# Attention scores in two passes over stacked rounded parts, part stores one chunk later in the queue, first head fetched a stage early, latent keys in two column tiles

## The chip, the cores and the metric

The kernel runs on one NeuronCore of a Trainium2 chip. The metric is the device time of one execution in microseconds (us), the median of the runs. TensorE multiplies matrices and writes to PSUM; VectorE, ScalarE and GpSimd work elementwise; SP's queue issues nearly all transfers. All data are 32-bit floats. A float32 product of TensorE is exact to float32 and leaves two records in the trace; a product on the rounded type float32r leaves one, and the kernel gets its precision back by cutting an operand into a rounded high part and the rounded rest (low part) and adding products of parts.

## The reference

Two transformer blocks run one after the other on x of 1024 tokens by 1024 channels. The first has differential and latent attention, a memory attention and a mixture of experts. What the change touches there is the up-projection of latent keys, `(_rms_norm(c_kv) @ w_mla_ukv)`, 8 heads of 64 key rows. The second block projects its normalised input with `w_in` into rows for four mixers and gates:

```python
fq, fk = rms_norm(fq, fox_q_gain), rms_norm(fk, fox_k_gain)         # 4 heads of 64
c = cumsum(log_sigmoid(f_logit))                                    # per head, over tokens
s = q @ k.T * d**-0.5 + (c[i] - c[j]); causal; softmax; @ v         # fox_attention
mlstm: (q @ k.T) * exp(decay), causal, 4 heads; sum over keys; rms_norm; * sigmoid(mo)
sq, sk = rms_norm(...)                                              # 8 query heads, 2 key heads
s = q @ k.T * d**-0.5 + bias, keys of the last 128 tokens; softmax with sink; @ v   # swa_attention
y_conv = short_conv_mixer(cu, cb, cc, conv_w)
g = sigmoid(gates); merged = sum over 4 branches of g * (y @ w_branch); x = x + merged @ w_merge
```

A SwiGLU feed-forward network ends the block.

## The kernel before, in words

P = 128, S = 1024, HD = 64, HALF = 512, ST = 8 token blocks of 128. Stages follow one another with a barrier between them. Three matter here.

`first_rows` (L1097) makes the rows of the first mixer. TensorE multiplies one chunk of 128 output rows after the other, each as 48 products of parts, and puts the work of one latent head into the middle of a chunk (`head`): four float32 products of 512 columns for the queries, into `q_ps` (L1250), two for the keys, into partitions 0 to 63 of `k_ps` (L1253). ScalarE copies both out (`leave_head`, L1317 and L1318).

`mixer_rows` (L2963) projects 22 chunks of 128 rows for the second block: chunk 0 the gate logits, 1 to 4 fox queries and keys, 5 to 9 window queries and keys (1 to 9 are normalised), 10 to 19 plain, 20 and 21 output gates. For chunk j ScalarE rounds the weights (`high_part`, L3168), VectorE makes the low part (`low_part`, L3227), TensorE runs 48 products into `acc[j % 2]` (L235 to L237). A normalised chunk is squared by ScalarE (L3179), TensorE sums the squares per head (L3111, in the middle of the next chunk), VectorE scales the mean (L3232), ScalarE takes logarithm and exponential (L3189, L3191), VectorE writes the chunk to `stage[j % 2]` (`normalise`, L3239), and TensorE waits for that before chunk j + 2. ScalarE's program for chunk j is: leave(j), rounding of the weights of j + 2, roots of j. VectorE's is: low part of the weights of j + 2, mean, normalise, then parts of the gate rows (`gate_step`, behind chunks 0, 5, 9 and 10) and sums of token blocks (`block_sum`, L3305). SP's program is the loop

```python
for j in range(2, N):
    load(j)              # waits for low part j - 2, then 512 KB of weights
    if j >= 3:
        store(j - 2)     # waits until chunk j - 2 is in its stage
```

with the stores of gate rows, window rows and token blocks between. GpSimd is idle in this stage after some fills.

`gated_attention` (L3654) runs 128 steps of one block of 128 queries: steps 0 to 31 fox heads, 32 to 63 recurrent (mLSTM) heads, 64 to 127 window heads, head g = step // 8. In one step TensorE makes the score of the block (`score`, L4000), transposes the exponentials of the step before, runs its share of the gate projection (`gates`, L235 to L237, some ten products of 512 columns) and multiplies with the values (L4020) or, for recurrent heads, adds up (L4031). A fox or recurrent score of block t is 128 by (t + 1) x 128 or S - t x 128 keys, a window score 128 by 256 (128 in block 0). It is float32, 64 channels and two more rows deep; for fox heads the two rows carry the running sum c of the query and of the key and ones, for others zeros, written once by GpSimd (L3970). The operands lie in `k.X` (`q_of`, `k_of`), in two sets by turns; `load_head(g)` (L3841) fills them through SP's queue, four transfers for fox heads and two for others, at step 8 (g - 1), after the scores of head g - 2. Head 0 and 1 and the gate memory `ml_y` are loaded at the start of the stage. VectorE shifts or weighs the scores (L4232, L4251), ScalarE exponentiates. SP also carries gate weights (L3861), gate stores and partial sums (L3883, L3891), convolution rows (L3919), token blocks (L3906) and the first two branch weights into `vm` (L3846, step 70).

`merge_branches` (L4360) follows and begins with the branch weights in `vm` and `fox_y`.

Of the kernel before, what the change touches and what calls it, by code (L numbers as in the profile page):

```python
# [22 lines left out]
F32 = mybir.dt.float32  # L23
# [96 lines left out]
class Core:  # L120


    def __init__(self, nc, ctx, dram, out, scratch):
# [29 lines left out]
        self.first_gate_in = ctx.enter_context(nc.semaphore("first_gate_in"))  # L153
        self.block_sums = ctx.enter_context(nc.semaphore("token_block_sums"))
# [13 lines left out]
        with ExitStack() as overlaid:  # L168
            self.sb("x_first_half", [P, ST // 2, D], ctx=overlaid)
            self.down_parts = pair(self, "moe_down_ws", [P, 2 * D], overlaid)  # L170
        self.X = sb("X", [P, ST, D])
# [925 lines left out]
def first_rows(k, H, vm, heads):  # L1097
# [4 lines left out]
    with k.phase() as ctx:  # L1102
# [119 lines left out]
        def _(pe):  # L1222
# [17 lines left out]
            def head(h):  # L1240
# [47 lines left out]
        def _(act):  # L1288
# [21 lines left out]
            def leave_head(h):  # L1310
# [6 lines left out]
                nc.scalar.activation(ks[b], k_ps[0:NOPE, :], ACT.Copy).then_inc(nopes, 1)  # L1317
# [1645 lines left out]
def mixer_rows(k, HT, vm, biases, sinks, spare, raw):  # L2963
# [11 lines left out]
    N_NORMED = 9  # L2975
    with k.phase() as ctx:
        weights = [pair(k, f"pr_ws{b}", [P, KD, P], ctx) for b in range(2)]
        stage = [k.sb(f"pr_stage{b}", [P, S], ctx=ctx) for b in range(2)]
# [10 lines left out]
        raws, logs, ones, a, top, floor, neg = ([k.X[0:H, c, :] for c in range(3)], [k.X[0:H, c, :] for c in (3, 4)],  # L2989
                                                k.X[0:H, 5, :], k.X[0:H, 6, :], k.X[0:H, 7, :],  # L2990
                                                spare[1][0:H, 0, :], spare[1][0:H, 1, :])
        totals = [spare[2][0:H, 0, :], spare[2][0:H, 1, :]]
        acc = [k.ps(f"pr_acc{b}", [P, S], ctx) for b in range(2)]
# [5 lines left out]
         wb_stored, wb_loaded, wb_turns, upright) = k.sems(  # L2999
            "pr", "cleared highs lows products left_normed left_plain stored0 stored1 squared summed meaned rooted bias_in "  # L3000
            "copied absed logged rows_made turned row_stored rel_in bucketed wb_made hot_made wb_product wb_rows "
            "wb_stored wb_loaded wb_turns upright")
# [22 lines left out]
        def _(sp):  # L3025
# [5 lines left out]
            def store(j):  # L3031
                sp.wait_ge(*left(j))
                sp.dma_start(chunks[j][2], stage[j % 2][:]).then_inc(stored[j % 2], 16)

            def store_rows():
                fox_q = k.scratch["fox_q"].rearrange("(h n) s -> h n s", n=2)
                fox_k = k.scratch["fox_k"].rearrange("(h n) s -> h n s", n=2)
                sp.wait_ge(cleared, 2)
                sp.dma_start(fox_q[:, 0, :], ones).then_inc(row_stored, 16)
                sp.dma_start(fox_k[:, 1, :], ones).then_inc(row_stored, 16)  # L3040
                sp.wait_ge(rows_made, 4)
# [2266 lines left out]
```

## Time and profile before

| what | value |
|---|---|
| median of 3 runs | 3204.66 us (3198.21 to 3834.82) |
| the profiled execution | 3198.8 us, span 3197.0 us |
| TensorE busy | 3001.7 us, 94% of the span |
| VectorE, ScalarE, GpSimd busy | 1985.1, 1567.1, 488.2 us |
| `mixer_rows` | about 1466 to 1752 us of the span |
| `gated_attention` | about 1752 to 2325 us of the span |

Busy time is the time in which an engine has an instruction under way; matmuls are pipelined, so the start-to-start distance of two tells what one costs, and its duration holds the way through the array too. PE is TensorE, PEld its weight loads, DVE is VectorE, ACT ScalarE, POOL GpSimd, SPq the queue of SP. "[9.85 <-PE x]" behind a row is idle time before it and what ended it.

### The profile page before, as it was taken

How to read it: one execution, taken by the hardware profiler on the slowest of the kernel's cores; microseconds unless marked ns; L12 is line 12 of the kernel's file. 1: busy time of each engine (PE TensorE's matmuls, PEld its weight loads, DVE VectorE, ACT ScalarE, POOL GpSimd, SP SyncE). 2: the span in 40 equal slices, each digit the busy share in tenths (PEclk: the TensorE clock that was granted, in tenths of full speed). 3: DMA queues.
4: the chain of work that ended last, by engine and by line, in shares of the span. 5: the costliest groups of instructions: out<-in, count | busy, mean ns of one | idle time of the engine just before them, and what ended most of it. 6: DMA issues, size and time to landing. Idle time of an engine off the chain costs nothing. (4 is left out here: it accounts for less than half of the span.)

```text
span 3197.0 us, 40651 instructions
## 1 busy us (share of the span) xinstructions
PE 3001.7 (94%) x14913; PEld 2468.0 (77%) x14913; DVE 1985.1 (62%) x2873; ACT 1567.1 (49%) x2494; POOL 488.2 (15%) x429
## 2 busy tenths in 40 slices
PE   7998999898969999969999999989999899999999
PEld 6766999686858878868777787778877778888887
DVE  4336888523678888873432434566576576666685
ACT  5225778533558888853521443344453432322443
POOL 0001210000133333220000110113300032222000
PEclk9999999899979999989999999999999999999999
DMA  3334221302168888772243433377664223333653
GB/s 113 85 122 125 60 60 31 112 20 102 66 248 294 298 287 299 248 236 66 79 133 98 114 99 109 106 233 219 193 240 151 79 80 103 111 113 116 230 159 112
DMA packets 299781, 459.71 MB, mean 144 GB/s; under 512 B 47799, under 2 KB 195326, under 8 KB 287042
## 3 DMA queue, kind: packets, MB, share of 16 engines
q1 hardware_dynamic: 274946, 411.72, 40.4%
q10 hardware_dynamic: 9088, 28.58, 2.3%
q0 software_dynamic: 15552, 16.82, 1.8%
q8 instruction: 121, 1.98, 0.3%
q14 instruction: 74, 0.61, 0.1%
HBM read 401.47 MB, written 118.98 MB: 163 GB/s over the span
## 5 line engine op out<-in xcount | busy, mean ns | idle before, releaser
L2850 DVE TENSOR_TENSOR moe_wgu_low<-moe_raw,moe_wgu_high 128x2048 fp32r<-128x2048 f32 x94 | 211.2, 2288 | 47.4 <-ACT moe_wgu_high L2787 45.3
L235 PE MATMUL ga_gate<-second_h_high,ga_ws_high 128*128 128x512 f32 x448 | 198.0, 442 | 12.6 <-DVE ga_ws_low L4189 10.4
L2787 ACT ACTIVATE moe_wgu_high<-moe_raw 128x2048 fp32r<-128x2048 f32 x92 | 171.2, 1909 | 20.2 <-ACT moe_y L2796 20.2
L237 PE MATMUL ga_gate<-second_h_high,ga_ws_low 128*128 128x512 f32 x448 | 180.7, 403 | 0.0
L236 PE MATMUL ga_gate<-second_h_low,ga_ws_high 128*128 128x512 f32 x448 | 179.7, 401 | 0.0
L235 PE MATMUL pr_acc<-second_h_high,pr_ws_high 128*128 128x512 f32 x336 | 138.6, 412 | 13.4 <-DVE pr_stage L3239 10.0
L235 PE MATMUL up_bank<-second_h_high,up_w_high 128*128 128x512 f32 x352 | 139.0, 395 | 8.9 <-DVE up_w_low L3520 7.3
L2958 POOL DMA_INDIRECT moe_rows<-scratch_ffn_rows,slot_of_block x47 | 110.5, 2351 | 223.2 <-PE moe_turned L2740 155.1
L236 PE MATMUL up_bank<-second_h_low,up_w_high 128*128 128x512 f32 x352 | 138.6, 394 | 0.0
L237 PE MATMUL up_bank<-second_h_high,up_w_low 128*128 128x512 f32 x352 | 138.4, 393 | 0.0
L237 PE MATMUL pr_acc<-second_h_high,pr_ws_low 128*128 128x512 f32 x336 | 132.3, 394 | 0.0
L236 PE MATMUL pr_acc<-second_h_low,pr_ws_high 128*128 128x512 f32 x336 | 131.9, 392 | 0.0
L3562 DVE TENSOR_TENSOR X<-X,up_bank 128x512 f32<-128x512 f32 x132 | 90.6, 687 | 63.2 <-PE up_bank L237 59.9
L4000 PE MATMUL ga_scores<-X 66*128 66x256 f32 (+3 forms) x320 | 119.8, 474 | 6.3 <-DVE swa_y L4251 6.0
L4215 DVE TENSOR_TENSOR ga_stage<-ga_stage,ga_gate 128x512 f32<-128x512 f32 x96 | 65.8, 685 | 88.5 <-PE ga_gate L237 68.6
L3227 DVE TENSOR_TENSOR pr_ws_low<-pr_w,pr_ws_high 128x1024 fp32r<-128x1024 f32 x22 | 26.9, 1228 | 148.4 <-ACT pr_ws_high L3168 148.4
L235 PE MATMUL down_acc<-second_h_high 128*128 128x512 f32 x300 | 116.7, 389 | 0.0
L236 PE MATMUL down_acc<-second_h_low,second_h_high 128*128 128x512 f32 x300 | 116.7, 389 | 0.0
L237 PE MATMUL down_acc<-second_h_high,second_h_low 128*128 128x512 f32 x300 | 116.7, 389 | 0.0
L1681 ACT ACTIVATE twin_pt<-twin_turned 128x512 f32<-128x512 f32 (+1 forms) x192 | 86.8, 487 | 58.2 <-PE twin_turned L1567 57.1
L2806 ACT ACTIVATE moe_down_ws_high<-moe_raw_down 128x1024 fp32r<-128x1024 f32 x94 | 99.7, 1061 | 31.4 <-PE moe_down L237 31.4
L4114 ACT ACTIVATE ga_row<-ga_turned 128x256 f32<-128x256 f32 (+4 forms) x96 | 44.4, 463 | 141.0 <-PE ga_turned L4010 140.8
(671 smaller groups left out, 8650.7 us busy)
## 6 DMA issues: line engine op xcount, KB each, us to landing
moe_raw<-in_w_expert_gate_dram SPq DMA_DIRECT2D x32, 1024.0 KB, 5.0
moe_raw<-in_w_expert_up_dram SPq DMA_DIRECT2D x32, 1024.0 KB, 7.2
moe_raw_down<-in_w_expert_down_dram SPq DMA_DIRECT2D x32, 1024.0 KB, 7.3
scratch_gates<-ga_stage SPq DMA_DIRECT2D x96, 256.0 KB, 2.5
scratch_expert_rows<-moe_y ACTq DMA_DIRECT2D x46, 512.0 KB, 4.8
ga_w<-in_w_in_dram SPq DMA_DIRECT2D x92, 256.0 KB, 3.6
scratch_hidden<-X SPq DMA_DIRECT2D x77, 256.0 KB, 2.1
down_rows<-scratch_hidden SPq DMA_DIRECT2D x73, 256.0 KB, 3.1
```

The source lines that it names most:

```text
L235: nc.tensor.matmul(out, w[0], x[0], start=start, stop=False)
L236: nc.tensor.matmul(out, w[0], x[1], start=False, stop=False)
L237: return nc.tensor.matmul(out, w[1], x[0], start=False, stop=stop)
L1681: nc.scalar.activation(turned_sb[p % 4][:, 0:end - start, :], turned[p % 2][:, 0:end - start, :], ACT.Copy).then_inc(copied, 1)
L2787: nc.scalar.activation(wgu[i % 2][0][:, :, m, :], raw[(2 * i + m) % RAW][:].rearrange("p (c n) -> p c n", n=FF), ACT.Copy).then_inc(up_hig ...
L2806: nc.scalar.activation(w_down[0][:, c * D:(c + 1) * D], raw_down[i % RAW_DOWN][:, c * D:(c + 1) * D], ACT.Copy).then_inc(down_highs, 1)
L2850: nc.vector.tensor_tensor(wgu[i % 2][1][:, :, m, :], raw[(2 * i + m) % RAW][:].rearrange("p (c n) -> p c n", n=FF), wgu[i % 2][0][:, :, m, ...
L2958: k.nc.gpsimd.indirect_dma_start(out=rows[i % 2][:], out_offset=None, in_=k.scratch["ffn_rows"], in_offset=bass.IndirectOffsetOnAxis(ap=sl ...
L3562: nc.vector.tensor_tensor(out, x, bank_at(f, bank_i), ALU.add).then_inc(combos, 1)
L4000: last = nc.tensor.matmul(scores[:, at:to], own[0:HD + 2, t * P:(t + 1) * P], other[0:HD + 2, key + at:key + to], start=True, stop=True)
L4114: nc.scalar.activation(pt[:, 0:chunks_of(n), :], turned[:, 0:chunks_of(n), :], ACT.Copy).then_inc(copied, 1)
L4215: nc.vector.tensor_tensor(stage[t][:], prior[:], bank[:], ALU.add).then_inc(added, 1)
```

## The change

Scores: query and key rows are stored as high and low parts. One operand tile holds high and low rows of one side stacked (128 rows), the other holds the high rows of the other side twice; their product is high x high + low x high. A second product, 68 rows deep, adds high x low and the four rows for the running sums (zeros where there are none). Both are float32r, into the same PSUM columns. The parts are made in `mixer_rows` by GpSimd, out of the stage, and stored by SP; `store(j - 3)` takes the place of `store(j - 2)` in its loop. Head 0 is fetched at the end of `mixer_rows`. The new tiles lie over `k.X`, `ml_y`, `vm` and `ga_row`, so `ml_y` is loaded at step 64 and the second branch weight after the last score. The fills of zero rows by GpSimd go.

```diff
@@ first_rows
                 for n in range(2):
-                    last = nc.tensor.matmul(k_ps[0:NOPE, n * HALF:(n + 1) * HALF], wn[:, h, :], latent[2][:, n * HALF:(n + 1) * HALF],
-                                            start=True, stop=True)
+                    last = nc.tensor.matmul(k_ps[n * NOPE:(n + 1) * NOPE, n * HALF:(n + 1) * HALF], wn[:, h, :],
+                                            latent[2][:, n * HALF:(n + 1) * HALF], start=True, stop=True)
...
-                nc.scalar.activation(ks[b], k_ps[0:NOPE, :], ACT.Copy).then_inc(nopes, 1)
+                for n in range(2):
+                    last = nc.scalar.activation(ks[b][:, n * HALF:(n + 1) * HALF], k_ps[n * NOPE:(n + 1) * NOPE, n * HALF:(n + 1) * HALF],
+                                                ACT.Copy)
+                last.then_inc(nopes, 1)
@@ mixer_rows
             def store(j):
-                sp.wait_ge(*left(j))
-                sp.dma_start(chunks[j][2], stage[j % 2][:]).then_inc(stored[j % 2], 16)
+                if j in split_no:
+                    sp.wait_ge(row_splits, 2 * split_no[j] + 1)
+                    sp.dma_start(chunks[j][2], high_rows[:].bitcast(F32)).then_inc(highs_stored, 16)
+                    sp.wait_ge(row_splits, 2 * split_no[j] + 2)
+                    sp.dma_start(low_rows[j], stage[j % 2][:].bitcast(F32)).then_inc(stored[j % 2], 16)
+                else:
...
-                if j >= 3:
-                    store(j - 2)
+                if j >= 4:
+                    store(j - 3)
...
+            store(N - 3)
+            load_first_head()
             store(N - 2)
             store(N - 1)
...
+            for j, n in split_no.items():
+                rows_of_chunk = stage[j % 2]
+                pool.wait_ge(*left(j))
+                if n:
+                    pool.wait_ge(row_splits, 2 * n)
+                    pool.wait_ge(highs_stored, 16 * n)
+                nc.gpsimd.tensor_copy(high_rows[:], rows_of_chunk[:].bitcast(F32)).then_inc(row_splits, 1)
+                pool.wait_ge(row_splits, 2 * n + 1)
+                nc.gpsimd.tensor_tensor(rows_of_chunk[:], rows_of_chunk[:].bitcast(F32), high_rows[:],
+                                        ALU.subtract).then_inc(row_splits, 1)
...
-                        v.tensor_scalar(neg, totals[0], -1.0, None, ALU.mult).then_inc(rows_made, 1)
+                        v.tensor_copy(total_high, totals[0]).then_inc(rows_made, 1)
+                        dve.wait_ge(rows_made, 2)
+                        v.tensor_tensor(total_low, totals[0], total_high, ALU.subtract).then_inc(rows_made, 1)
@@ gated_attention, load_head(g)
                 if g >= 2:
                     sp.wait_ge(products, ST * (g - 1))
+                if g == 8:
+                    sp.wait_ge(exps, 7 * ST)
+                if g == 12:
+                    sp.wait_ge(values, 8 * ST)
...
+                sources = [(own[0:HD, :], highs_of[own_at:own_at + HD, :]), (own[HD:2 * HD, :], lows_of[own_at:own_at + HD, :])]
+                if g < 8 or g % 4 == 0:
+                    sources += [(other[0:HD, :], highs_of[other_at:other_at + HD, :]),
+                                (other[HD:2 * HD, :], highs_of[other_at:other_at + HD, :]),
+                                (other_low[0:HD, :], lows_of[other_at:other_at + HD, :]),
+                                (other_low[HD:HD + 4, :], k.scratch["fox_k"][h * 4:h * 4 + 4, :] if g < 4 else k.scratch["zero_rows"])]
+                if g < 4:
+                    sources += [(own_again[0:HD, :], highs_of[own_at:own_at + HD, :]),
+                                (own_again[HD:HD + 4, :], k.scratch["fox_q"][h * 4:h * 4 + 4, :])]
...
-            load_head(0)
-            load_head(1)
-            sp.dma_start(ml_y[:, :, :], k.scratch["mo"].rearrange("(c p) s -> p c s", p=P)).then_inc(mo_in, 16)
             for a in (A11, A22):
                 load_quarter(1, a)
             for q in range(RING):
                 load_quarters(q)
+            load_head(1)
...
+                if s == 64:
+                    sp.wait_ge(products, 8 * ST)
+                    sp.dma_start(ml_y[:, :, :], k.scratch["mo"].rearrange("(c p) s -> p c s", p=P)).then_inc(mo_in, 16)
                 if s == 70:
-                    load_branches()
+                    load_branch(0)
+                if s == N + 1:
+                    load_branch(1)
@@ gated_attention, score(n)
                 for at in range(0, width, HALF):
                     to = min(at + HALF, width)
-                    last = nc.tensor.matmul(scores[:, at:to], own[0:HD + 2, t * P:(t + 1) * P], other[0:HD + 2, key + at:key + to],
-                                            start=True, stop=True)
+                    nc.tensor.matmul(scores[:, at:to], own[:, t * P:(t + 1) * P], other[:, key + at:key + to],
+                                     start=True, stop=False)
+                    last = nc.tensor.matmul(scores[:, at:to], own_again[0:HD + 4, t * P:(t + 1) * P],
+                                            other_low[0:HD + 4, key + at:key + to], start=False, stop=True)
```

`split_no` holds chunks 1 to 9 and 16 to 19. `load_first_head` issues the eight transfers of head 0, after waits for the stores of chunks 1 to 4 and for the gate rows. The stored gate rows are ten transfers for five.

## Rows read from the trace of the kernel before

**Rows 1.** Busy time of each engine in four stretches: us, busy, clock, DMA share.

```profile
1757.00:1910.00 153.00, 150.79 (x819) 120.83 (x818) 65.03 (x121) 67.09 (x132) 22.05 (x19) 1.00 0.38 107
1910.00:2065.00 155.00, 148.96 (x728) 117.59 (x727) 75.01 (x142) 63.77 (x116) 15.61 (x12) 0.93 0.38 107
2065.00:2315.00 250.00, 235.76 (x1217) 196.69 (x1217) 149.70 (x301) 104.25 (x270) 69.90 (x52) 0.97 0.72 213
1500.00:1745.00 245.00, 231.64 (x970) 180.99 (x969) 91.32 (x64) 82.77 (x79) 0.00 (x0) 0.98 0.35 108
```

**Rows 2.** Waits of TensorE, 1500 to 1752 us: in total, times, longest.

```profile
PE pr_acc L235 <- DVE pr_stage L3239: 10.0, 7, 5.4
PE pr_acc L235 <- DVE pr_ws_low L3227: 3.4, 2, 2.1
```

**Rows 3.** Waits of TensorE, 2066 to 2318 us.

```profile
PE ga_gate L235 <- DVE ga_ws_low L4189: 4.7, 3, 3.7
```

**Rows 4.** Forms of the score products: count | busy us, mean ns | idle before.

```profile
L4000 PE MATMUL ga_scores<-X 66*128 66x512 f32 x96 | 51.8, 635 | 6.0 <-DVE swa_y L4251 6.0
L4000 PE MATMUL ga_scores<-X 66*128 66x256 f32 x144 | 46.8, 407 | 0.2 <-DVE ga_least L4232 0.2
L4000 PE MATMUL ga_scores<-X 66*128 66x384 f32 x32 | 15.2, 562 | 0.0
L4000 PE MATMUL ga_scores<-X 66*128 66x128 f32 x48 | 10.1, 291 | 0.0
```

**Rows 5.** TensorE in order of time, fox heads: start us, us.

```profile
1867.34 1.94 PE L4000 MATMUL ga_scores<-X 66*128 66x512 f32 x4
1869.11 0.93 PE L4010 MATMUL ga_turned<-ident,ga_p 128*128 128x128 f32 x7
...
1878.42 0.65 PE L4000 MATMUL ga_scores<-X 66*128 66x256 f32 x2
1878.91 0.28 PE L4010 MATMUL ga_turned<-ident,ga_p 128*128 128x128 f32 x1
```

**Rows 6.** TensorE in order of time, rounded score products of the first mixer.

```profile
336.76 0.60 PE L1555 MATMUL twin_scores<-mix_h_low 96*128 96x256 f32 x3
337.20 0.49 PE L1567 MATMUL twin_turned<-ident,twin_latent 128*128 128x128 f32 x3
...
339.03 0.71 PE L1555 MATMUL twin_scores<-mix_h_high 96*128 96x512 f32 x2
339.58 0.60 PE L1567 MATMUL twin_turned<-ident,twin_first 128*128 128x128 f32 x4
...
340.83 0.53 PE L1555 MATMUL twin_scores<-mix_h_low 96*128 96x128 f32 x3
341.19 0.41 PE L1567 MATMUL twin_turned<-ident,twin_latent 128*128 128x128 f32 x2
```

**Rows 7.** ScalarE, TensorE and VectorE in order of time, row projections.

```profile
1541.69 1.06 ACT L3168 ACTIVATE pr_ws_high<-pr_w 128x1024 fp32r<-128x1024 f32 x1 [4.66 <-DMA pr_w<-in_w_in_dram]
...
1603.02 0.47 PE L235 MATMUL pr_acc<-second_h_high,pr_ws_high 128*128 128x512 f32 x1 [0.29 <-DVE pr_stage L3239]
...
1607.22 1.88 PE L3111 MATMUL pr_sums<-pr_square,ones 128*128 128x512 f32 x4
...
1617.85 0.47 PE L235 MATMUL pr_acc<-second_h_high,pr_ws_high 128*128 128x512 f32 x1 [1.90 <-DVE pr_stage L3239]
...
1611.70 1.22 DVE L3232 TENSOR_SCALAR pr_norm<-pr_sums 128x1024 f32<-128x1024 f32 x1
```

**Rows 8.** GpSimd and VectorE in order of time, first mixer.

```profile
317.24 1.03 POOL L1535 CAST mix_h_low<-mix_h_low 96x1024 fp32r<-96x1024 f32 x1 [29.58 <-DMA mix_h_high<-scratch_qk]
...
318.36 2.39 POOL L1537 TENSOR_TENSOR mix_h_low<-mix_h_low 96x1024 fp32r<-96x1024 f32 x1
...
318.78 2.24 DVE L1629 SCALAR_TENSOR_TENSOR twin_first<-twin_second,twin_factor,twin_first 128x256 f32<-128x256 f32 x1
```

**Rows 9.** TensorE in order of time, latent keys.

```profile
144.70 1.93 PE L1253 MATMUL fr_k<-X,fr_wn 128*64 128x512 f32 x4
```

More of the change, by code:

```diff
@@ L170, in __init__ @@
             self.down_parts = pair(self, "moe_down_ws", [P, 2 * D], overlaid)
+        with ExitStack() as overlaid:
+            self.x_rounded = [self.sb(f"x_rounded{c}", [P, S], F32R, overlaid) for c in range(ST)]
         self.X = sb("X", [P, ST, D])
@@ L2988, in mixer_rows @@
         flipped = spare[0].rearrange("p c (h n) -> p (c h) n", n=2 * P)
-        raws, logs, ones, a, top, floor, neg = ([k.X[0:H, c, :] for c in range(3)], [k.X[0:H, c, :] for c in (3, 4)],
+        raws, logs, ones, a, top, floor, minus = ([k.X[0:H, c, :] for c in range(3)], [k.X[0:H, c, :] for c in (3, 4)],
                                                 k.X[0:H, 5, :], k.X[0:H, 6, :], k.X[0:H, 7, :],
@@ L3031, in store @@
             def store(j):
-                sp.wait_ge(*left(j))
-                sp.dma_start(chunks[j][2], stage[j % 2][:]).then_inc(stored[j % 2], 16)
-            def store_rows():
[L3036 to L3041, printed above, removed]
-                sp.dma_start(fox_q[:, 1, :], totals[0]).then_inc(row_stored, 16)
-                sp.dma_start(fox_k[:, 0, :], neg).then_inc(row_stored, 16)
-                sp.dma_start(k.scratch["mlstm_row"], top).then_inc(row_stored, 16)
+                if j in split_no:
[4 more added lines that the diff above has]
+                else:
+                    sp.wait_ge(*left(j))
+                    sp.dma_start(chunks[j][2], stage[j % 2][:].bitcast(F32)).then_inc(stored[j % 2], 16)
@@ new lines, in load_first_head @@
+            def load_first_head():
+                qk, low, (own_at, key_at) = k.scratch["fox_qk"], k.scratch["fox_qk_low"], (0, 256)
+                own, keys, keys_low, own_again = k.x_rounded[4], k.x_rounded[5], first_lower, k.x_rounded[2]
+                sp.wait_ge(turned, 1)
+                sp.wait_ge(row_stored, 16 * 10)
+                sp.wait_ge(highs_stored, 16 * 4)
+                for stored_of in stored:
+                    sp.wait_ge(stored_of, 16 * 2)
+                for tile, source in ((own[0:HD, :], qk[own_at:own_at + HD, :]), (own[HD:2 * HD, :], low[own_at:own_at + HD, :]),
+                                     (keys[0:HD, :], qk[key_at:key_at + HD, :]), (keys[HD:2 * HD, :], qk[key_at:key_at + HD, :]),
+                                     (keys_low[0:HD, :], low[key_at:key_at + HD, :]),
+                                     (keys_low[HD:HD + 4, :], k.scratch["fox_k"][0:4, :]),
+                                     (own_again[0:HD, :], qk[own_at:own_at + HD, :]),
+                                     (own_again[HD:HD + 4, :], k.scratch["fox_q"][0:4, :])):
+                    sp.dma_start(tile.bitcast(F32), source).then_inc(k.first_fox_head_in, 16)
@@ L3666, in gated_attention @@
         probs = [k.sb(f"ga_p{b}", [P, S], ctx=ctx) for b in range(2)]
+        with ExitStack() as overlaid:
+            lower = [*lower, k.sb("ga_lower3", [P, S], F32R, overlaid)]
         row = [k.sb(f"ga_row{b}", [P, S], ctx=ctx) for b in range(2)]
@@ L3729, in head_target @@
         def head_target(g):
-            loads = sum(4 if h < 4 else 2 for h in range(g % 2, g + 1, 2))
-            return 16 * loads
+            if g == 0:
+                return k.first_fox_head_in, 16 * 8
+            loads = sum(8 if h < 4 else 6 if h < 8 or h % 4 == 0 else 2 for h in range(2 - g % 2, g + 1, 2))
+            return head_in[g % 2], 16 * loads
         first_four, last_three = (A11_B11, A12_B21, S2_T2, S1_T1), (A22_T4, S3_T3, S4_B22)
@@ L4973, in second_mixer @@
         conv_y = up_first[:, :, :, :].rearrange("p m c n -> p m (c n)")
+        with ExitStack() as overlaid:
+            lower = [k.sb(f"ga_lower{b}", [P, S], F32R, overlaid) for b in range(2)]
         ml_y = k.sb("ml_y", [P, 2, S], ctx=ctx)
```

105 lines of the change are left out of this document (60 added, 45 removed).

## The prediction

> **What bounds the kernel now.** I read the table of stretches first. In the decaying attention (fox) heads TensorE is busy 150.8 of 153 us, in the recurrent heads 149.0 of 155, in the window heads 235.8 of 250, and in the row projections 231.6 of 245; VectorE, ScalarE and GpSimd are far from full in all four [rows 1]. So in these stages a shorter TensorE program shortens the kernel, as long as no wait takes the place of it. The waits say where TensorE stands still: in the projections 10.0 us for the normalised chunk and 3.4 us for low weights [rows 2]; in the window heads 4.7 us for gate weights, 3.7 of it in one piece [rows 3]. Last I read the forms of the score products and the order of time around them, for what one costs.
>
> **Scores, what goes.** 160 score products leave 320 records: 48 of 512 columns, 72 of 256, 16 of 384, 24 of 128, halved from the counts [rows 4]. Start to start of the next piece of work, a 1024-wide row block takes 1869.11 - 1867.34 = 1.77 us and a 256-wide one 1878.91 - 1878.42 = 0.49 [rows 5]. That is 0.213 us for each further 128 columns, so 0.28, 0.49, 0.70, 0.92, 1.13, 1.35, 1.56 and 1.77 for the eight widths.
>
> **Scores, what comes.** Two rounded products per piece. The first mixer already runs such products, 96 rows deep: two of 512 columns take 339.58 - 339.03 = 0.55, three of 256 take 0.44, three of 128 take 0.36 [rows 6]. Three of 128 cost nearly as much as three of 256, so below 256 columns the weight load sets the pace and a narrow product gains nothing. One less of the narrow ones is 0.11: two of 128 make 0.25, two of 256 make 0.33, two of 384 (halfway) 0.44, and wider ones add to 0.55 a piece: 0.79, 0.76, 0.87, 0.98 for 640 to 1024 (the last is 0.55 plus two more of 0.215). The saving by width is 0.03, 0.16, 0.26, 0.37, 0.34, 0.59, 0.69, 0.79: 3.23 us for a fox or recurrent head, times 8 is 25.8; a window head has seven 256-wide blocks and one 128-wide, 1.15 us, times 8 is 9.2. Together 35.0 us. Part of it falls into the stages at granted clock 0.93 and 0.97 [rows 1], where it is worth 1.3 us more. Depth 128 or 68 in place of 96 and 66 I take to cost nothing: at depth 66 a pass streams 128 columns in 0.213 / 4 = 0.053 us, at depth 96 in 0.055 or so (0.55 for 1024), so depth shows in neither. Bounds: 52,224 columns at two passes less each, at 2.4 GHz, are 43.5 us; if only the 512-wide and 384-wide pieces gained, it is 48 x 0.37 + 16 x 0.26 = 22 us.
>
> Does it stay? In the fox heads nothing else is near full, so yes. In the recurrent heads four waits of 1.5 us for a weighting stay, as they hang on the head before. In the window heads VectorE chains (division, convolution) stop TensorE now and again, and the DMA engines are busy 0.72 [rows 1]; a chain that ended in time may now end late. I take 2 us off: 34 us is left.
>
> **What the scores bring with them.** A fox head loads 8 tiles for 4, a recurrent head 6 for 2, window heads 0 and 4 load 6 for 2: 40 more issues on SP of about 0.45 us, spread over 560 us in which SP mostly waits, and some 9 MB more over queues at 0.38 in the first two stages. Hidden, as heads are asked for a head ahead; behind them in SP's queue stand gate weights, which have a step or more of room. The gate memory (1024 KB, four times a gate weight) moves to step 64, its first use being at step 72, some 30 us later. The new waits of SP there (exponentials of step 55, values and scores of step 63) are over, or nearly, when SP comes to them, since the head load just ahead waits for the same scores. The second branch weight is now issued after the last gate store, some 3 us before the stage ends; in the merge it is the second of two and the first keeps TensorE busy for 5 us. I take 1 us for all of this, and 0 to 6 as its bounds (6 is one more stall like that of 3.7 us [rows 3] and a late branch weight). Head 0 fetched early takes away a wait of 0.4 us before the first score. The four fills on GpSimd that go were off the path.
>
> **Row projections.** This is the part that I weigh highest after the scores. Before, SP stands at the store of chunk j - 2 and only then issues the load of chunk j + 1. So the weights are asked for when the chunk is already running, and ScalarE waits 4.66 us for them and can round them only at 1541.69 [rows 7]; behind that in ScalarE's and VectorE's queues stand the mean, the logarithm, the exponential and the normalised chunk that TensorE waits for. With stores one chunk later in the queue the load is issued a chunk earlier and has landed. Then the chain is: the sums of squares end at 1607.22 + 1.88 - 1603.02 = 6.1 us into the chunk, so the mean may begin at 6.2; from its begin to TensorE's next chunk it is 1617.85 - 1611.70 = 6.15; 12.35 in all, against 1617.85 - 1603.02 - 1.90 = 12.93 of TensorE's own work [rows 7]. The waits for chunks (10.0) and for low weights (3.4) go [rows 2], the longest of the first (5.4) because 2 MB of kept token blocks no longer stand between weights and chunk. A mean granted clock of 0.98 over 245 us [rows 1] is, at the two levels 1.2 and 2.4 GHz, some 10 us at half clock, 5 us lost, which follow the longest waits; I take 3.2 of them. What can go is 16.6 us.
>
> Against it stands the new work of GpSimd. Each of 13 chunks gets a rounding copy and a subtraction over 1024 columns, 1.03 and 2.39 us by the same pair in the first mixer [rows 8], 3.4 us of a chunk's 12.9. They are not free for VectorE: its operation on two SBUF tiles, 256 wide, that begins at 318.78 while GpSimd's subtraction runs ends only with it, after 2.24 us [rows 8]. The Trainium skill, GPSIMD Engine Reference, section Specifications, has the rule for this: GpSimd and VectorE share SBUF interfaces, and VectorE operations with two SBUF inputs contend; by that rule, and the trace agrees, the low weights and the block sums are held, while the mean and the normalisation, which read PSUM, are not. In an ordinary chunk block sum, both GpSimd operations and low weights, one after another, are 2.3 + 3.4 + 1.2 = 6.9 us against the 6.2 at which the mean may begin, 0.1 us past the slack of 0.6. In chunk 5 the running sum of the forget gate stands there too, and now one operation more (1.2 + 2.3 + 0.5 + 1.0 + 2.3 + 1.2 = 8.5 us, up to 11.9 with GpSimd): 2 to 5 us of wait, of which I take 3.5. SP now waits for GpSimd's halves before each load, 3.5 us behind the chunk; the load still has 9 us and needs 5. So 16.6 - 3.5 - 1 = 12 us. Bounds 4 and 16.6.
>
> **Latent keys.** Four records of 512 columns now take 1.93 us, the last one's way out of the array included, in one set of array columns [rows 9]. After, the second half writes the other 64 output partitions. The records stay in order, two for each half, and two of one half can't overlap each other; the first of the second half can run beside the second of the first. That is three slots for four: 0.46 us a head, 3.7 for eight, all on TensorE's path, as its chunks follow each other there. No row shows two column tiles at once, so the bounds are 0 and 7.4 (both halves wholly side by side). ScalarE's copy becomes two and costs a few tenths, beside TensorE's chunk. The Trainium skill, TensorEngine Tiling (Array Packing), Key Properties, says that different tiles can load and multiply in parallel; by that alone it would be 7.4 us.
>
> **Sum.** 34 + 0.4 - 1 + 12 + 3.7 = 49 us. The profiled execution took 3198.8 us with a span of 3197.0, so 3150 for it. It was the quickest but one beside the runs shown (3198.2 and 3204.7, and one far above), and their median stands 6 us over it; I put the forecast at 3152.
>
> **Rivals.**
> (a) All terms at their good end: 43 + 16.6 + 7.4 + 0.4 = 67 us, 3134. For it: the columns; against: the narrow rows [rows 6], and 0.36 for three narrow products can't be argued away.
> (b) The scores gain, the projections don't: GpSimd's hold on VectorE and SP's wait for it eat what the earlier loads give. 34 + 3.7 - 1 + 0 to 4, about 3162. For it: the hold [rows 8] is real and the slack in a chunk only 0.6; against: the held operations come before the mean may begin.
> (c) The window heads become bound by the DMA engines and VectorE, so 9.2 us there and some in the recurrent heads are lost: about 3165. For it: the share of 0.72 and the stall of 3.7 us; against: TensorE runs without a wait over the last third at the same share.
> (d) Slower than before: the splits on GpSimd set the pace of the projections. It decides from the point where copy, subtraction and both stores take longer than the 12.9 us of a chunk less the 5 us of a load, so from about 8 us a chunk instead of 4.5. At 12 us a chunk, 13 chunks lose 4 us each, 52 us, and take the whole gain back; at the 14 us that GpSimd would need if each of its operations waited out the whole of VectorE's and it were held twice, the kernel is at 3152 + 78 = 3230. The rows give 3.4 us, so it is unlikely.
> (e) The change doesn't do what it says: the products on the newly typed tiles run at four passes as before. Then each score costs twice its price now, 87 us more against 15 gained, 3273. The rounded products of the first mixer read tiles filled by DMA too, so I hold this for nearly excluded.
>
> **Chances.** Forecast 0.62, (a) 0.12, (b) 0.10, (c) 0.12, (d) and (e) 0.04. The likeliest one's own range is 3140 to 3162. The range of 3131 to 3178 takes in (b), (c) and most of (a). Two per cent, about what a measurement of this kernel can tell from no change, is 64 us, so a time of 3140 or less: all of (a) and a small part of the forecast, 0.15. Slower by as much only with (e) and the far end of (d), 0.02. Within, 0.83.
>
> **What would show it.** Scores: 640 records, two 512-wide ones at 0.55 us from start to start, 256-wide blocks at 0.33, TensorE's busy time in the three attention stages down by some 35 us and the fox stage by 12 to 13. Projections: ScalarE no longer waits for weights ahead of the rounding, the waits of TensorE for chunks down from 10 to about 4 us, most of it in one place, low weights that last up to 3 us in places where 1.2 was the rule. Latent keys: records of the second half starting beside those of the first, 1.5 us in place of 1.93. Wrong: a wait of TensorE for DMA'd head tiles, waits for gate weights above 8 us in the window heads, or waits for chunks still at 10.

## The result, and the profile after

The changed kernel takes 3152.85 us (median of 4 runs) against 3206.89 for the kernel before (4 runs). Of the fast runs alone, without one of 3834.82 us of the kernel before, the ratio is 0.9865, with a 95% interval of [0.9838, 0.9893]: shorter, clear of noise, by less than 2%. The forecast was 3152, range 3131 to 3178. The profiled executions have spans of 3150.6 and 3197.0 us, a difference of 46.4.

First look: where in the span the 46.4 us went. I cut both traces at the same events: first and last key product (`fr_k`), first and last row projection product (`pr_acc`), first gate product, first and last weighting of a recurrent head, last gate product (`ga_gate`). The forecast of each stretch is its terms of the prediction's sum; the 1.3 us for the lower clock are all put to the recurrent heads here.

| stretch, us | before | after | gain | forecast |
|---|---|---|---|---|
| latent keys, first to last | 115.2 | 108.4 | 6.8 | 3.7 |
| from there to the row projections | 1219.2 | 1217.6 | 1.6 | 0 |
| row projections | 268.3 | 257.5 | 10.8 | 12 |
| fox heads (to the first weighting) | 165.4 | 152.0 | 13.4 | 12.9 |
| recurrent heads (to the last weighting) | 142.5 | 126.9 | 15.6 | 14.2 |
| window heads (to the last gate product) | 259.2 | 258.5 | 0.7 | 7.2 |
| all else | | | -2.5 | -0.6 |

So the total was right by compensation: the keys gave nearly twice their estimate, and the window heads next to nothing. That one line is what most of the experiments are about.

The second look is the view of stretches, cut at these events, for the kernel before (columns as in [rows 1]: length; busy time of TensorE, its weight loads, VectorE, ScalarE, GpSimd; granted clock; DMA share; GB/s):

```profile
1479.10:1747.40 268.30, 254.94 (x1069) 199.56 (x1067) 96.97 (x70) 92.74 (x88) 0.00 (x0) 0.98 0.32 99
1919.30:2061.80 142.50, 136.63 (x650) 107.31 (x651) 71.41 (x136) 57.52 (x105) 15.61 (x12) 0.93 0.38 105
2061.80:2321.00 259.20, 244.96 (x1269) 204.62 (x1268) 155.12 (x311) 106.08 (x274) 69.90 (x52) 0.97 0.70 208
```

and for the changed one, which answers to [rows 1]:

```profile
1470.30:1727.80 257.50, 252.64 (x1068) 199.71 (x1067) 109.13 (x71) 92.13 (x88) 70.83 (x26) 0.99 0.41 129
1734.70:1886.70 152.00, 149.16 (x880) 130.11 (x880) 66.53 (x127) 73.42 (x142) 21.48 (x18) 0.99 0.50 134
1886.70:2013.60 126.90, 118.36 (x651) 102.33 (x652) 70.80 (x135) 56.91 (x104) 15.88 (x12) 0.97 0.52 142
2013.60:2272.10 258.50, 237.61 (x1269) 201.63 (x1268) 152.73 (x312) 105.76 (x275) 70.53 (x52) 0.95 0.71 214
```

In the window heads TensorE's busy time did fall, 244.96 to 237.61, 7.4 us. The stretch did not: TensorE's idle time (length less busy time) rose from 14.2 to 20.9 us and the granted clock fell from 0.97 to 0.95.

Who let TensorE wait there? The waits of VectorE say it; first the kernel before (2061 to 2321 us), then the changed one (2013 to 2272), for us in total, times, longest:

```profile
DVE ga_stage L4215 <- PE ga_gate L237: 39.0, 36, 2.0
DVE ga_p L4232 <- PE ga_scores L4000: 26.3, 26, 2.6
DVE ga_stage L4215 <- DMA ga_stage<-scratch_gates: 19.5, 7, 5.8
```

```profile
DVE ga_stage L4283 <- DMA ga_stage<-scratch_gates: 35.8, 12, 8.3
DVE ga_stage L4283 <- PE ga_gate L240: 29.3, 29, 3.0
```

A gate is summed up from several products; its partial sum is stored to DRAM and fetched back for the next one. VectorE waits for these reloads: 19.5 us before, 35.8 after. I had read only TensorE's waits in this stretch [rows 3], in which these hide under names such as low weights and shifts. In order of time, around the longest of them in the changed kernel (start, duration, engine, line; SPq is SyncE's queue of DMA issues):

```profile
2137.74 2.49 SPq L3956 DMA_DIRECT2D scratch_gates<-ga_stage  x2
...
2146.49 0.32 SPq L3964 DMA_DIRECT2D ga_stage<-scratch_gates  x1
...
2149.68 0.69 DVE L4283 TENSOR_TENSOR ga_stage<-ga_stage,ga_gate 128x512 f32<-128x512 f32 x1 [8.33 <-DMA ga_stage<-scratch_gates]
...
2150.28 0.69 DVE L4257 TENSOR_TENSOR ga_ws_low<-ga_w,ga_ws_high 128x512 fp32r<-128x512 f32 x1
2150.89 0.48 DVE L4300 CUSTOM_DVE_ANT_0 ga_p<-ga_scores,up_raw,ga_neg_sinks 128x256 f32<-128x256 f32 x1
```

The chain is: two tiles are stored at 2137.74; SyncE stands at L3964 until the store has landed and issues the reload of the same tile only at 2146.49; it is there some 3 us later; behind the sum in VectorE's queue stand the low weights and the shift for which TensorE waits. One tile goes through store, landing, reload, landing in every round of three gate products. At this line SyncE waits 76.5 us in all before and 81.7 us after for stores to land, so the queue held the reloads up in the kernel before as well.

In the row projections ScalarE's waits for weights, which the new order was to take away, went from 62.2 us in 11 waits to 11.6 in 4. The first row is ScalarE's in the kernel before (1500 to 1752 us); the waits of TensorE that answer to [rows 2], in the changed one (1400 to 1720 us), are the other two:

```profile
ACT pr_ws_high L3168 <- DMA pr_w<-in_w_in_dram: 62.2, 11, 11.1
```

```profile
PE pr_acc L238 <- DVE pr_stage L3291: 4.1, 1, 4.1
PE pr_acc L238 <- DVE pr_ws_low L3279: 0.8, 1, 0.8
```

and the longer one stands where the prediction put it, behind the running sum of the forget gate (VectorE, then GpSimd, in order of time):

```profile
1543.45 1.28 DVE L3291 SCALAR_TENSOR_TENSOR pr_stage<-pr_acc,head_gains,pr_norm 128x1024 f32<-128x1024 f32 x1 [3.50 <-ACT pr_norm L3243]
...
1545.89 3.01 DVE L3307 TENSOR_TENSOR_SCAN swa_y<-X 4x1024 f32<-4x1024 f32 x1
1548.93 2.68 DVE L3311 CAST x_rounded<-swa_y 4x1024 fp32r<-4x1024 f32 x1
...
1556.13 1.21 DVE L3284 TENSOR_SCALAR pr_norm<-pr_sums 128x1024 f32<-128x1024 f32 x1
```

```profile
1544.80 1.97 POOL L3151 CAST pr_high_rows<-pr_stage 128x1024 fp32r<-128x1024 f32 x1 [6.13 <-DVE pr_stage L3291]
1546.85 4.22 POOL L3153 TENSOR_TENSOR pr_stage<-pr_stage,pr_high_rows 128x1024 fp32r<-128x1024 f32 x1
```

From the normalised chunk to the next mean it is 12.7 us; the mean stands behind all of it. Note the gap of 3.50 us ahead of the normalisation, in which VectorE does nothing. GpSimd's pair of operations took 70.83 / 13 = 5.4 us a chunk in this stage, where the prediction had 3.4.

Score products, answering to [rows 5], a 256-wide block of the window heads:

```profile
2097.29 0.36 PE L4066 MATMUL ga_scores<-x_rounded 128*128 128x256 f32 x1
2097.49 0.28 PE L4068 MATMUL ga_scores<-ga_lower,x_rounded 68*128 68x256 f32 x1
2097.62 0.38 PE L4078 MATMUL ga_turned<-ident,ga_p 128*128 128x128 f32 x2
```

2097.62 - 2097.29 = 0.33 us, the price forecast for it. (The prediction looked for 640 records of scores. That is a wrong count: 160 pieces of two products with one record each are 320, and 320 are in the trace.)

### The profile page after: what moved, and what is told of

It reads as the page before. It is cut to its first block and busy times, and to the rows that moved or that the text cites. A ratio compares the mean times of both kernels' runs of the same rounds, so it can differ in the third digit from the quotient of the medians.

```text
span 3150.6 us, 40756 instructions
## 1 busy us (share of the span) xinstructions
PE 2950.7 (94%) x14913; PEld 2454.7 (78%) x14913; DVE 1993.9 (63%) x2874; ACT 1568.3 (50%) x2502; POOL 557.5 (18%) x452
## 5 line engine op out<-in xcount | busy, mean ns | idle before, releaser
L238 PE MATMUL ga_gate<-second_h_high,ga_ws_high 128*128 128x512 f32 x448 | 190.2, 425 | 15.2 <-DVE ga_ws_low L4257 12.2
L238 PE MATMUL pr_acc<-second_h_high,pr_ws_high 128*128 128x512 f32 x336 | 137.8, 410 | 4.9 <-DVE pr_stage L3291 4.1
L238 PEld LDWEIGHTS ga_gate<-second_h_high,ga_ws_high 128*128 128x128 f32 x448 | 87.2, 195 | 32.1 <-DVE ga_ws_low L4257 13.5
L2867 DVE TENSOR_TENSOR moe_down_ws_low<-moe_raw_down,moe_down_ws_high 128x1024 fp32r<-128x1024 f32 x94 | 110.6, 1217 | 1.8 <-ACT moe_down_ws_high L2812 1.7
L238 PE MATMUL up_bank<-up_t_high,up_w_high 128*128 128x512 f32 x264 | 103.0, 390 | 1.4 <-DVE up_w_low L3574 1.4
```

Of the source, the lines that this page charges most:

```text
L238: nc.tensor.matmul(out, w[0], x[0], start=start, stop=False)
L2867: nc.vector.tensor_tensor(w_down[1][:, c * D:(c + 1) * D], raw_down[i % RAW_DOWN][:, c * D:(c + 1) * D], w_down[0][:, c * D:(c + 1) * D], ...
```

## The experiments

Whole times vary more than some of these effects: the 1217.6 us between keys and row projections, which no edit touches, were 1218 to 1227 in most of the later profiles and 1245 in one. So each experiment is read from its own stretch, in one profile, and the ratio of whole times to the kernel before is given beside it. Where the edits leave a stretch of the changed kernel alone, its profiles agree within 0.1 us for the keys, 1.2 for the row projections (256.4 to 257.6), 0.7 for the fox heads, 3.5 for the recurrent heads, and 6.7 for the window heads (257.0 to 263.7 in six profiles).

**Latent keys.** The edit puts the second half of the keys back on the first 64 output partitions, and the single copy with it:

```diff
-  nc.tensor.matmul(k_ps[n * NOPE:(n + 1) * NOPE, n * HALF:(n + 1) * HALF], wn[:, h, :], ...)
+  nc.tensor.matmul(k_ps[0:NOPE, n * HALF:(n + 1) * HALF], wn[:, h, :], ...)
```

> The changed kernel with its latent keys in one column tile and one ScalarE copy again, nothing else altered. Measured on the stretch from TensorE's first key product to its last (115.2 us before, 108.4 after). Theory 1, two column tiles run wholly side by side and all of the gain comes from them: the stretch goes back to 115, the four records to 1.86 us, the kernel is 6 to 7 us longer. Theory 2, my three slots for four: only 3.7 us of the gain belong to the tiles, the stretch is near 112 and some 3 us come from something else.

The stretch was 115.2 us (145.1 to 260.3); the ratio 0.9879 [0.9863, 0.9896]. TensorE in order of time, the changed kernel first, then this one:

```profile
144.31 1.08 PE L1256 MATMUL fr_k<-X,fr_wn 128*64 128x512 f32 x4
145.32 0.50 PE L238 MATMUL fr_acc<-mix_h_high,fr_ws_high 128*128 128x512 f32 x1
```

```profile
145.08 1.93 PE L1256 MATMUL fr_k<-X,fr_wn 128*64 128x512 f32 x4
146.94 0.50 PE L238 MATMUL fr_acc<-mix_h_high,fr_ws_high 128*128 128x512 f32 x1
```

Four records hold TensorE for 1.01 us in two column tiles and 1.86 in one: the halves run side by side but for 0.08 us (half of 1.86 is 0.93), and eight heads at 0.85 us each are all of the 6.8. This is what the Trainium skill states in TensorEngine Tiling (Array Packing), Key Properties, that different tiles load and multiply at the same time.

**Row projections: order alone, splits alone, and a third layout.** The order alone, on the kernel before (with the store of N - 3 added ahead of the last two):

```diff
-                if j >= 3:
-                    store(j - 2)
+                if j >= 4:
+                    store(j - 3)
```

> The kernel of before with the stores of the row projections one chunk later in SP's queue and nothing else of the change: no splits on GpSimd. Measured from TensorE's first row projection product to its last (268.3 us before, 257.5 in the changed kernel). Theory 1, as predicted, the order is worth up to 16.6 us and the splits take 4 to 5 of them back: 252 us here, TensorE's waits for chunks and low weights nearly gone. Rival, the splits cost nothing and the order is worth only what the changed kernel shows: 257 us, with a wait of about 4 us still there behind the running sum of the forget gate.

The same two lines the other way round on the changed kernel:

> The changed kernel with the stores of the row projections back at their old place in SP's queue (store of chunk j - 2 behind the load of chunk j, one chunk earlier than in the change), the splits on GpSimd kept. Theory 1: SP now waits for GpSimd's two operations (some 3.5 to 7 us) and the two stores before each load, weights come as much later, and each of the 13 split chunks loses about 3 us: from the first row projection product to the last 290 to 315 us, most of TensorE's new waits for low weights. Rival: the splits cost only their hold on VectorE, so 268.3 + 4.5 = 273 us.

And the changed kernel with VectorE's side work moved into the gap:

```diff
                 if chunks[j][0] == normed:
                     mean(j)
...
+                if j == 5:
+                    gate_step(1)
+                if j == 6:
+                    split_total()
+                if 2 <= j <= 8 and j not in (5, 6):
+                    block_sum(j - 2)
                 if chunks[j][0] == normed:
                     normalise(j)
-                if j == 5:
-                    gate_step(1)
+                if j in (5, 6):
+                    block_sum(j - 2)
```

(`split_total` is the rounding and the rest of the running sum, taken out of `gate_step`; block sums 0 to 6 no longer stand at the end of their chunk.)

> The changed kernel with VectorE's side work of the row projections (block sums, running sum of the forget gate, its rounding and rest) moved into the gap of 3.5 us between the mean and the normalisation, in which VectorE waits for ScalarE, and the rounding and rest of the running sum one chunk later; GpSimd's split then meets less of it. Theory 1, the wait of 4.1 us behind the running sum and the 0.8 for low weights come from these operations standing ahead of the next mean: both go, the stretch of row projections is 257.5 - 5 = 252 to 253 us. Rival 1, the gap is too short and the normalised chunk comes late in its place: 257 us or more, with TensorE waiting for pr_stage in several chunks. Rival 2, the rest of the stretch is TensorE's own work at its granted clock and the wait only moves: 256 to 257.

The stretches in these three, by the view of stretches, in the order order alone, splits in the old order, side work in the gap:

```profile
1479.50:1729.40 249.90, 249.81 (x1069) 198.04 (x1068) 97.44 (x70) 92.00 (x88) 0.00 (x0) 1.00 0.32 98
```

```profile
1477.50:1795.80 318.30, 272.51 (x1068) 212.10 (x1068) 105.47 (x71) 92.15 (x88) 65.70 (x26) 0.90 0.34 110
```

```profile
1480.20:1730.70 250.50, 249.79 (x1069) 197.87 (x1068) 109.00 (x71) 92.18 (x88) 56.62 (x26) 1.00 0.42 131
```

The order alone gives 268.3 - 249.9 = 18.4 us, a little more than the 16 expected; TensorE has no wait left and a clock of 1.00, and ScalarE's waits for weights are down to 3.2 us (ratio 0.9954 [0.9937, 0.997]). The splits take back 257.5 - 249.9 = 7.6. The rival of no cost is out.

In the old order the splits cost 50.0 us (318.3 against 268.3), 3 more than the upper end of what I expected, and the kernel is slower than before, 1.0055 [1.0038, 1.0072]. Of the 50.0 us, 32.4 are idle time of TensorE and 17.6 are its own work at a clock of 0.90 for 0.98. The first row is SyncE's wait there, the second ScalarE's, the third TensorE's:

```profile
SPq L3046 <- POOL pr_high_rows L3150: 193.7, 13, 33.7
...
ACT pr_ws_high L3219 <- DMA pr_w<-in_w_in_dram: 116.0, 11, 17.0
...
PE pr_acc L238 <- DVE pr_stage L3290: 37.7, 8, 8.8
```

SyncE's wait holds the time until the chunk itself is ready too (in the changed kernel this wait is 116.9 us). In the old order this wait comes before SyncE asks for the next weights: ScalarE can't round them, and the mean and normalisation behind that in the queues come late. TensorE waits for the chunk (37.7 us) more than for low weights (8.1), which my expectation had the other way. So the kernel gets slower as rival (d) of the prediction says, but in the old order and at 65.70 / 13 = 5.1 us of GpSimd's work a chunk, not the 8 named there: what decided was where in SyncE's queue the wait for it stands.

With the side work in the gap, splits kept, the stretch is 250.5 us, 7.0 less, and TensorE's two waits are down to one of 0.7; I had expected 252 to 253 us (ratio 0.9831 [0.9815, 0.9848]). So it isn't the length of the splits that costs, but that they meet work of VectorE which stands ahead of the next mean. VectorE in the kernel with the order alone, at the same place, and the rounding of the running sum in the one with the gap:

```profile
1552.65 1.28 DVE L3240 SCALAR_TENSOR_TENSOR pr_stage<-pr_acc,head_gains,pr_norm 128x1024 f32<-128x1024 f32 x1 [3.50 <-ACT pr_norm L3192]
...
1555.09 2.28 DVE L3256 TENSOR_TENSOR_SCAN swa_y<-X 4x1024 f32<-4x1024 f32 x1
...
1561.34 1.21 DVE L3233 TENSOR_SCALAR pr_norm<-pr_sums 128x1024 f32<-128x1024 f32 x1
```

```profile
1562.41 0.67 DVE L3296 CAST x_rounded<-swa_y 4x1024 fp32r<-4x1024 f32 x1
```

8.7 us to the next mean without splits, 12.7 with: the scan takes 3.01 for 2.28, the rounding 2.68 where it takes 0.67 undisturbed, and the subtraction of 1.21 is new. The 7.6 us are 4.8 more of idle time (257.5 - 252.64 against 249.9 - 249.81) and 2.8 more of busy time, for work that is the same at a clock of 0.99 against 1.00.

**Window heads: is TensorE the bound?** One edit, with two conditions:

```diff
-  nc.tensor.matmul(scores[:, at:to], own[...], other[...], start=True, stop=False)
-  last = nc.tensor.matmul(scores[:, at:to], own_again[...], other_low[...], start=False, stop=True)
+  once = kind_of(n) == "window"        # the other kernel: == "fox"
+  last = nc.tensor.matmul(scores[:, at:to], own[...], other[...], start=True, stop=once)
+  if not once:
+      last = nc.tensor.matmul(scores[:, at:to], own_again[...], other_low[...], start=False, stop=True)
```

The window kernel leaves out high x low. The fox kernel leaves out the running sums as well, whose four rows are in the same product. Both serve for their times alone.

> The changed kernel with the second score product left out in the window heads (the correction of the rounded keys is not computed there). That takes 72 products of 128 or 256 columns off TensorE, some 8 to 10 us of its time. Measured from the first window shift of VectorE to the last product with gate weights (251.1 us before, 250.4 after). Theory 1, the window heads are paced by the store and reload of partial gates, which all pass through SP's queue: the stretch shrinks by less than 3 us, VectorE's waits for reloaded partials grow. Theory 2, TensorE's program sets the pace: it shrinks by 8 us or more.

> The changed kernel with the second score product left out in the fox heads alone (the correction of the rounded keys is not computed there). 48 products, 8 at 128 and the rest 256 to 512 columns wide, go: half of what two passes cost, 4 x (0.25 + 0.33 + 0.44 + 0.55 + 0.79 + 0.76 + 0.87 + 0.98) / 2 = 10 us at most. Theory 1, the fox heads are bound by TensorE: the stretch from the first gate product to the first recurrent weighting (165.4 us before, 152.0 after) shrinks by 7 to 10 us. Theory 2, there as in the window heads another chain has become the bound: under 3 us.

Window heads: from the last weighting, 258.1 us against 258.5 (from the first shift, as in the expectation, 250.1 against 250.4), although TensorE's busy time fell by 7 us (230.63 against 237.61); the ratio is that of the change, 0.9865 [0.9833, 0.9897]. VectorE's waits for reloads were 44.2 us, but they were 42.6 in a second profile of the changed kernel too, so a rise is not shown. Fox heads: 143.1 against 152.0, 8.9 us less, as expected (0.9821 [0.9805, 0.9837]). So TensorE bounds the fox heads and, within the spread of that stretch, not the window heads. (In the fox kernel the window stretch was 263.7 us; that is within its spread, not a gain given back, as the expectation of the run with both edits below has it.)

**Window heads: the round trip.** The tile of two weightings of recurrent heads, `ga_w_rest`, is free in the window heads. It takes every other one of the reloads that are summed first in a round, and these reloads are issued one gate product earlier; tile and earlier issue go together and are not told apart here:

```diff
+        stage.append(w_rest)
...
-            return {S2_T2: 2, A12_B21: 3, S3_T3: 3, A22_T4: 2}.get(i, m % 2)
+            return {S2_T2: 2, A12_B21: 3, S3_T3: 3, A22_T4: 2 if m % 2 == 0 else 4}.get(i, m % 2)
...
-                if i == S4_B22 and m + 1 < 2 * PAIRS:
+                if i == S3_T3 and m + 1 < 2 * PAIRS:
                     load_partial(m + 1, A22_T4)
```

(and semaphores and counts to match; nothing else is altered.)

> The changed kernel with a second tile for the reloaded partial gate that is summed first in each round, taken from a tile that is free in the window heads; its reload is issued one gate step earlier and no longer waits for the store of the round before. Nothing is computed otherwise. Theory 1, the round trip store, landing, reload, landing on one tile stops VectorE, behind it the low weights and the shifts, and so TensorE: VectorE's waits for the reloads (35.8 us, 12 times) fall to under 10 us and the window stretch of 250.4 us loses 6 to 10 us. Theory 2, these waits have cover enough and the window heads are bound by other chains (division, convolution, DMA load of the engines): under 2 us.

> The kernel of before with the second tile for reloaded partial gates alone. Measured from the last recurrent weighting to the last gate product (259.2 us before, 258.5 in the change, 244.7 in the change with the tile). Theory 1, my 9.2 us for the window scores were right and the round trip took them back: the tile gives the kernel of before only what it waited there already, and the stretch is 244.7 + 9.2 = 254 us. Theory 2, the round trip bound the window heads before in the same way and the scores are worth nothing there at all: 245 us here too. Theory 3, the round trip became a bound only with the change: 259 us, no gain.

The changed kernel with the tile: 244.7 us, 13.8 less (6 to 10 expected) and 12.3 below the shortest of the six profiles without it; VectorE's waits for reloads 35.8 to 5.8 us, SyncE's for stores to land 81.7 to 20.6, ratio 0.9823 [0.9805, 0.9841]. VectorE's waits for reloads that are left:

```profile
DVE ga_w_rest L4286 <- DMA ga_w_rest<-scratch_gates: 3.1, 1, 3.1
DVE ga_stage L4286 <- DMA ga_stage<-scratch_gates: 2.7, 1, 2.7
```

The kernel before with the tile, window heads:

```profile
2065.70:2316.20 250.50, 241.69 (x1268) 202.75 (x1268) 155.43 (x311) 106.27 (x274) 71.06 (x52) 0.98 0.71 215
```

259.2 (260.0 in a second profile without the tile) to 250.5, with no wait of VectorE for a reload left, ratio 0.9978 [0.9956, 1.0], a gain of the whole that is not clear of noise. The stretch is at neither 254 nor 245 us: the round trip held the window heads back by 8.7 us before the change already, and by 13.8 or more after it. With the tile in both, TensorE's busy time falls by 241.69 - 231.88 = 9.8 us at the same clock of 0.98, near the 9.2 of the sum, and the stretch by 250.5 - 244.7 = 5.8 us, or by 10.7 against the next kernel with the tile (239.8, below). So the scores are worth about the 7.2 forecast here, within a spread of 5 us, and the round trip took it.

**All together.**

> The changed kernel with both edits: VectorE's side work in the gap of the row projections, and the second tile for reloaded partial gates. Each gave its stage 7.0 us (257.5 to 250.5) and 13.8 us (258.5 to 244.7, last recurrent weighting to last gate product). Theory 1, the stages follow one another and the gains add: both stretches as in the single runs, 3152.9 - 20.8 = 3132 us, a ratio to before near 0.977. Theory 2, an earlier stage that ends sooner gives the window heads nothing, as the gain of 8.9 us in the fox heads was half lost there (263.7 us): near 3139.

> The changed kernel as it is, on the same chip as the others of this call, for comparison with them. Every theory: stretches of 257.5 us in the row projections and 258.5 in the window heads, within 2 us, and a ratio to before near 0.986.

> The changed kernel with both edits and with the second score product left out in the window heads (the correction of the rounded keys is not computed there). With the one reload tile the same cut gave 0.4 us (258.5 to 258.1). Theory 1, with the round trip out of the way the window heads are bound by TensorE again: 5 to 8 us off 244.7, so 237 to 240. Theory 2, the second tile only moved the bound to another chain (divisions, gate memory times rows, stores): 243 or more.

On one chip: both edits 3130.29 us (6 runs), ratio 0.9774 [0.9745, 0.9802]; both edits with one pass in the window heads 3125.60, 0.9758 [0.9721, 0.9794]; the changed kernel 3155.52, 0.9848 [0.9818, 0.9878]; the kernel before 3200.43. The gains add: 3155.52 - 3130.29 = 25.2 us for 7.0 + 13.8 = 20.8 in single runs, and the row projections took 250.8 us. Window heads with both edits, the changed kernel again, and both edits with one pass:

```profile
2008.50:2248.30 239.80, 229.23 (x1268) 195.48 (x1267) 155.37 (x312) 105.71 (x275) 72.30 (x52) 0.99 0.75 231
```

```profile
2014.20:2277.00 262.80, 239.25 (x1269) 201.90 (x1268) 153.28 (x312) 105.40 (x275) 71.52 (x52) 0.95 0.70 211
```

```profile
2006.30:2241.30 235.00, 221.52 (x1205) 187.77 (x1204) 151.46 (x312) 105.92 (x275) 72.53 (x52) 0.99 0.77 236
```

The changed kernel's window stretch was 4 us longer than in its first profile, outside the 2 us that I had allowed. Leaving the second product out takes 7.7 us of busy time off TensorE and now 4.8 us off the stretch (it was 0.4 with the one tile): a little less than the 5 to 8 expected, and the 235.0 lies below the 237 to 240, as both edits alone were at 239.8 and not at 244.7. TensorE is the main bound again, at a clock of 0.99.

## Why the prediction was right, and where it was not

- **Scores, 34 us: 29.7 came.** Fox 13.4 for 12.9; recurrent 15.6 for 12.9 and 1.3 of clock. The latter is partly luck of the profile of before: the same stretch, untouched, took 139.4 and 137.8 us in two other kernels built on it, at a clock of 0.95 and 0.96 for 0.93, so the gain there is nearer 11 to 13. Window heads 0.7 for 7.2: here the step failed that kept 9.2 us less 2 for "a chain that ended in time may now end late". The chain was in the trace of before already, 19.5 us of VectorE's waits for reloaded gates, and I didn't look behind the names in TensorE's waits. Rival (c) was right in effect for this stretch, and right that VectorE stops TensorE, but the cause is not the share of DMA: with the second tile the share goes up, to 0.75, and the time down.
- **Row projections, 12 us: 10.8 came**, from two terms that were both too small. The order was worth 18.4, not 16.6. The splits took back 7.6, not 4.5: the waits fit (3.5 and 1 taken, 4.1 and 0.8 measured), but the clock that they cost, 2.8 us, was not in the sum.
- **Latent keys, 3.7 us: 6.8 came.** "Three slots for four" was wrong: I had kept the order of the records as a limit, and no such limit shows in 1.01 us for four.
- **Extra loads, 1 us:** no wait of TensorE for a head tile is in the trace, and the merge starts 8.1 us after the last gate product against 7.7 before; the term held. The 0.4 us for fetching head 0 early doesn't show: the first score starts 0.4 us after the gate product ahead of it in both traces.
- The rest, 1.6 us gained in the middle and 2.5 lost behind the last gate product, I leave unexplained; both stretches varied by that or more between profiles (the latter 875.7 to 878.6 us).

The change came within 2%, which had a chance of 0.83; one result can't test a chance. What the sum did not deserve is the credit for each term: the keys' 3.1 us too many stand against 6.5 too few in the window heads.

## What to carry to other kernels

Before a saving on the busiest engine is counted in full, read the waits of the other engines in that stretch as well, and follow the longest to the DMA behind it: what a queue holds up shows under the names of what stands behind it. A tile that is stored and reloaded in each round wants a partner, so that the reload doesn't wait for the store's landing. In an engine's own program, put side work into the gaps in which it waits for another engine, not between the last result and the next one that the bound engine needs.

## What the runs showed of the hardware that I had not expected

- Float32 products in two column tiles of 64 overlap almost wholly: 1.01 us for four of 512 columns against 1.86, at depth 128.
- GpSimd and VectorE hold each other in single-input operations too: VectorE's rounding of 4 partitions took 2.68 us beside GpSimd's subtraction and 0.67 without, and GpSimd's own pair 1.97 and 4.22 us where it took 1.03 and 2.39 [rows 8], and 1.04 and 2.41 for the first chunk of the same stage. In the prediction I counted only operations with two SBUF inputs. The Trainium skill, SBUF — State Buffer, Who interferes with whom, names copies and casts among those that can take the pair of ports that VectorE shares with GpSimd, and the trace agrees: 2.68 against 0.67 us.
- Short waits cost twice: in the row projections in the old order, 32.4 us more of idle time came with 17.6 more of busy time for the same work, at a clock of 0.90 for 0.98; in the window heads 6.7 us more idle time came with a clock of 0.95 for 0.97, and taking the waits away brought it to 0.98 and 0.99.
